# Hybrid streaming encoder step on one core: the last superchunk of the down projection in six, sixteen and six units, its norm on two engines, and the norm's shift added in memory

## The reference

```python
h = x @ w_in                       # branches: RG-LRU, band attention, forgetting attention
y = concat(rms(y_A), rms(y_B), rms(y_C))
x = LN1(ALPHA * x + y @ w_out)
hdn = square(relu(x @ w_up))       # 2048 -> 8192
out = LN2(ALPHA * x + hdn @ w_down)   # 8192 -> 2048; LN(v) = (v - mean) * rstd * g + b
```

## Time and profile before

| | us |
|---|---|
| median of 3 runs | 2359.68 (2357.44 to 2361.64) |
| profiled execution | 2353.08 |
| its span | 2351.3 |
| TensorE busy | 2294.7 (98%) |
| VectorE busy | 1558.3 (66%) |
| ScalarE busy | 955.2 (41%) |
| POOL busy | 264.1 (11%) |
| granted TensorE clock, mean | 0.995 |

### The profile page before, as it was taken

The page is one execution under the profiler, slowest core; times in us unless marked ns, Lnnn a source line. Parts: engine busy times, 40 slices in busy tenths (PEclk is TensorE's granted clock), DMA queues, the critical chain, the costliest instruction groups (busy, mean ns, idle before and its releaser), DMA issues. The chain is left out here.

```text
span 2351.3 us, 39849 instructions
## 1 busy us (share of the span) xinstructions
PE 2294.7 (98%) x16967; PEld 2250.5 (96%) x16967; DVE 1558.3 (66%) x1181; ACT 955.2 (41%) x957; POOL 264.1 (11%) x296
## 2 busy tenths in 40 slices
PE   7999999999999999999999999999999999998986
PEld 7999999999888999999999999999999999998985
DVE  3311455533457676667777777778778778778868
ACT  3222344423445354654444444455245235234332
POOL 2010233300011202200000000002112112111100
PEclk9999999999999999999999999999999999999998
DMA  7264333344643567775445555579689689769873
GB/s 211 82 193 128 104 101 101 97 153 132 194 150 109 162 207 231 215 245 191 154 156 182 160 178 182 170 236 239 174 238 247 180 235 238 197 184 273 205 224 117
DMA packets 383510, 421.99 MB, mean 179 GB/s; under 512 B 13716, under 2 KB 359512, under 8 KB 382824
## 3 DMA queue, kind: packets, MB, share of 16 engines
q1 hardware_dynamic: 319936, 335.73, 45.4%
q0 software_dynamic: 27552, 48.17, 10.8%
q10 hardware_dynamic: 35912, 36.49, 4.5%
HBM read 339.47 MB, written 82.45 MB: 179 GB/s over the span
## 5 line engine op out<-in xcount | busy, mean ns | idle before, releaser
L2506 PE MATMUL psum<-x_e_hi,w_hi 128*128 128x288 f32 x1600 | 471.4, 295 | 8.6 <-DVE w_lo L1703 7.0
L2506 PE MATMUL psum<-x_e_lo,w_hi 128*128 128x288 f32 x1600 | 472.7, 295 | 0.0
L2506 PE MATMUL psum<-x_e_hi,w_lo 128*128 128x288 f32 x1600 | 472.2, 295 | 0.0
L2506 PE MATMUL psum<-x_b_hi,w_hi 128*128 128x288 f32 x1536 | 452.9, 295 | 6.8 <-DVE w_lo L1821 2.7
L2506 PE MATMUL psum<-x_b_lo,w_hi 128*128 128x288 f32 x1536 | 453.8, 295 | 0.0
L2506 PE MATMUL psum<-x_b_hi,w_lo 128*128 128x288 f32 x1536 | 453.5, 295 | 0.0
L440 DVE TENSOR_TENSOR w_lo<-raw,w_hi 128x2048 fp32r<-128x2048 f32 x64 | 152.4, 2382 | 277.1 <-ACT w_hi L436 276.5
L2506 PEld LDWEIGHTS psum<-x_e_hi,w_hi 128*128 128x128 f32 x1600 | 301.5, 188 | 10.5 <-DVE w_lo L1703 8.6
L2506 PEld LDWEIGHTS psum<-x_e_lo,w_hi 128*128 128x128 f32 x1600 | 301.4, 188 | 0.0
L2506 PEld LDWEIGHTS psum<-x_e_hi,w_lo 128*128 128x128 f32 x1600 | 301.4, 188 | 0.0
L2506 PEld LDWEIGHTS psum<-x_b_hi,w_hi 128*128 128x128 f32 x1536 | 289.5, 188 | 8.9 <-DVE w_lo L1821 3.5
(11 more groups left out here) (390 smaller groups left out, 3786.4 us busy)
## 6 DMA issues: line engine op xcount, KB each, us to landing
raw<-in_w_down SPq DMA_DIRECT2D x62, 1024.0 KB, 7.1
raw<-in_w_up SPq DMA_DIRECT2D x54, 1024.0 KB, 6.6
raw<-in_w_in SPq DMA_DIRECT2D x40, 1024.0 KB, 5.3
a_even<-in_w_down SPq DMA_DIRECT2D x30, 1024.0 KB, 7.3
raw<-in_w_out SPq DMA_DIRECT2D x24, 1024.0 KB, 5.4
a_even<-in_w_up SPq DMA_DIRECT2D x24, 1024.0 KB, 6.7
h_scratch<-c_tile ACTq DMA_DIRECT2D x48, 288.0 KB, 2.8
down_scratch<-c_tile POOLq DMA_DIRECT2D x44, 288.0 KB, 5.7
```

What stands on the lines that cost most here:

```text
L2506: mm = pe.matmul(PS[:, bank, 0:HALF], w, x[:, k, :], start=(k + n == 0), stop=(k == UK - 1 and n == 2))
```

## The change

The last superchunk gets six first units, of which the last two take F2 for column blocks 0 and 1 (P_F), and six last units (P_E). Their weights, copies and accumulates follow; the load of S10F moves behind those of the first units 1 and 2. In the last block `lo_e(0)` comes ahead of the combination of HE1, and the combination after the two additions into Y1. Transposes follow half units instead of whole ones. `shift` is gone: VectorE makes `gain`, ScalarE multiplies by rstd (`scale`), and the shift ln2_b is written early, broadcast, to y_prompt and y_sample by two DMAs on ScalarE's queue; the rows are then accumulated onto it by POOL's DMAs.

```diff
-N_E = N_F + 5 * N_BLOCK
+N_E = N_F + 6 + 4 * N_BLOCK
-AFTER = ((0, 1, 2), (3, 4, 5), (6, 7), (8, 9), (10,), (11, 12), (13,), (14,))
+AFTER = (((0,), (1, 2)), ((3,), (4, 5)), ((6,), (7,)), ((8,), (9,)), ((10,), (11,)), ((12, 13), (14,)))
+P_F = ((0, 0), (0, 1), (0, 2), (0, 3), (1, 0), (1, 1))
+P_E = ((0, 2), (0, 3), (1, 0), (1, 1), (1, 2), (1, 3))
...
         def tile_e(v):
-            return 4 * (v % 4) + 2 * (v // 4)
+            return 4 * P_E[v][1] + 2 * P_E[v][0]
+        def tile_f(a):
+            return tile_a(N_SUPER, a, 0) if a < 4 else (CQ[a % 2], cd_out[a % 2], 16 * (7 * N_SUPER + 2))
...
@@ sync
             sp.dma_start(HB01[:, :, :], h_factor(0, 1, su)).then_inc(part_in[1], 16)
-            sp.wait_ge(lo_done, n + 1 + 3)
-            sp.wait_ge(sig, 4 * g + 4)
             sp.wait_ge(unit_done, n + 2 + 3)
             sp.dma_start(HE7[:, :, :], h_factor(1, 1, su)).then_inc(part_in[2], 16)
-            sp.dma_start(S10F[0][:, :, :], down_unit(1, 0, su, 0)).then_inc(a10_in, 16)
             sp.wait_ge(lo_done, n + 4 + 3)
             weights_f(1)
             sp.wait_ge(lo_done, A + 3)
             weights_f(2)
-            sp.dma_start(S11[0][:, :, :], down_unit(1, 1, su, 0)).then_inc(a11_in, 16)
+            sp.dma_start(S10F[0][:, :, :], down_unit(1, 0, su, 0)).then_inc(a10_in, 16)
             sp.wait_ge(lo_done, A + 1 + 3)
             weights_f(3)
+            sp.wait_ge(sig, 4 * g + 4)
+            sp.dma_start(S11[0][:, :, :], down_unit(1, 1, su, 0)).then_inc(a11_in, 16)
             sp.wait_ge(lo_done, A + 2 + 3)
+            weights_f(4)
+            sp.wait_ge(lo_done, A + 3 + 3)
+            weights_f(5)
+            sp.wait_ge(lo_done, A + 4 + 3)
             sp.dma_start(A00[:, :, :], down_unit(0, 0, su, 0)).then_inc(a00_in, 16)
...
             sp.wait_ge(unit_done, n + 2 + 3)
-            load_y0(0)
             sp.wait_ge(lo_done, N_E + 3)
             weights_e(2)
-            load_y0(1)
+            load_y0(2)
             sp.wait_ge(lo_done, N_E + 1 + 3)
             weights_e(3)
-            load_y0(2)
             load_y0(3)
-            for v in range(4, 8):
+            for v in (4, 5):
                 sp.wait_ge(lo_done, N_E + v - 2 + 3)
                 weights_e(v)
-            for n in range(4):
...
-                sp.dma_start(y_prompt[128 * t:128 * t + 128, c], ROWS_0[:, t, c]).then_inc(out_rows, 16)
+                load_y0(v - 4)
@@ scalar
             act.dma_start(s_fl, LFT[0:DEC, 4, :]).then_inc(stores, 16)
+            act.dma_start(y_prompt, ln2_b.to_broadcast([SEQ, D])).then_inc(shift_out, 16)
+            act.dma_start(y_sample, ln2_b.to_broadcast([DEC, D])).then_inc(shift_out, 16)
...
-            for a in range(4):
+            for a in range(6):
                 g, n, _ = block_f(0)
-                if a < 2:
+                if a < 4:
                     hi_a(su, a + 2)
                 else:
-                    hi_1b(n + a - 2, a % 2, (SIG2F, S10F[1])[a % 2], 4 * g + (2, 1)[a % 2])
-                tile, out, free_at = tile_a(su, a, 0)
+                    hi_1b(n + a - 4, a % 2, (SIG2F, S10F[1])[a % 2], 4 * g + (2, 1)[a % 2])
+                tile, out, free_at = tile_f(a)
...
+            def scale(h, t, c=slice(0, D)):
+                act.wait_ge(row_rs, 2 - h)
+                act.wait_ge(row_g, 3 * (1 - h) + t + 1)
+                w, r = ROW_T[t][1], row_tile(h, t)[:, c]
+                act.activation(r, r, ACT.Identity, scale=RST[0:w, 3 * h + t:3 * h + t + 1]).then_inc(row_y, 1)
-            for v in range(8):
-                if v < 6:
-                    hi_e(v + 2)
+            for v in range(6):
                 if v == 3:
                     row_sds(1, 1)
-                for s in AFTER[v]:
+                for s in AFTER[v][0]:
                     rows_copy(s)
+                if v < 4:
+                    hi_e(v + 2)
+                else:
+                    scale(1, v - 4)
+                for s in AFTER[v][1]:
+                    rows_copy(s)
+            scale(1, 2)
             rows_copy(15)
             row_sds(2, 0)
+            for t in range(2):
+                for n in range(2):
+                    scale(0, t, slice(D // 2 * n, D // 2 * (n + 1)))
+            scale(0, 2)
@@ vector
             combine(e1, e1, b01, 4 * su + 7)
+            lo_a(su, 4)
+            factor_rest(F6, HE6, 7 * su + 12)
+            lo_a(su, 5)
             dve.wait_ge(unit_done, N_F + 2)
             sigma1_f(g, 0)
+            factor_rest(F5, HE1, 7 * su + 13)
             sigma2_f(g, 0)
-            factor_rest(F6, HE6, 7 * su + 12)
+            factor_rest(F7, HE7, 7 * su + 11)
             lo_1b(n, 0, SIG2F)
-            factor_rest(F5, HE1, 7 * su + 13)
             sigma3_f(g, 0)
             lo_1b(n + 1, 1, S10F[1])
-            factor_rest(F7, HE7, 7 * su + 11)
...
                 else:
-                    dve.wait_ge(part_in[3], 16 * (2 * su + 3))
-                    combine(HE1[:, :, :], HE1[:, :, :], HB10_F[:, :, :], 4 * su + 8, minus=True)
-                    lo_e(0)
                     dve.wait_ge(part_in[0], 16 * (su + 3))
                     dve.wait_ge(post, p + 3)
                     dve.tensor_tensor(Y1[:, 14:16, :], Y1[:, 14:16, :], CQ[1][:, :, :], ALU.add).then_inc(y1_added, 1)
+                    lo_e(0)
...
                     dve.tensor_tensor(Y1[:, 12:14, :], Y1[:, 12:14, :], CQ[0][:, :, :], ALU.add).then_inc(y1_added, 1)
+                    dve.wait_ge(part_in[3], 16 * (2 * su + 3))
+                    combine(HE1[:, :, :], HE1[:, :, :], HB10_F[:, :, :], 4 * su + 8, minus=True)
                     lo_e(1)
                     factor_rest(F4F, HE1, 7 * su + 14)
...
+            for v in range(3):
+                add_y0(v)
+                lo_e(v + 2)
+                for s in ((0,), (1, 2, 3), (4, 5, 6))[v]:
                     row_stats(s)
+            row_stats(7)
+            row_means(1, 1)
+            add_y0(3)
+            lo_e(5)
+            row_rstd(1, 1)
+            dve.wait_ge(gb_in, 16)
+            gain(1, 0)
+            row_stats(8)
+            add_y0(4)
+            gain(1, 1)
+            row_stats(9)
+            row_stats(10)
+            gain(1, 2)
+            for s in range(11, 14):
+                row_stats(s)
+            add_y0(5)
+            row_stats(14)
             row_stats(15)
             row_means(2, 0)
-            gain(0, 0).then_inc(row_g, 1)
+            gain(0, 0)
             row_rstd(2, 0)
+            gain(0, 1)
+            gain(0, 2)
@@ gpsimd
             pool.dma_start(GR[:, :], ln2_g.to_broadcast([128, D])).then_inc(gb_in, 16)
-            pool.dma_start(BR[:, :], ln2_b.to_broadcast([128, D])).then_inc(gb_in, 16)
+            pool.wait_ge(shift_out, 32)
+            def add_out_rows(h, t, n, dst, p0=0, p1=None, c=slice(0, D)):
+                p1 = ROW_T[t][1] if p1 is None else p1
+                pool.wait_ge(row_y, n)
+                pool.dma_start(dst[:, c], row_tile(h, t)[p0:p1, c], accum_op=ALU.add).then_inc(out_rows, 16)
...
@@ tensor
+                    for s in AFTER[v][m]:
+                        rows_transposed(s)
```

More of the change, by code:

```diff
@@ L352, in encoder_step @@
         stats_done, row_sd, row_rs = sem("stats_done"), sem("row_sd"), sem("row_rstd")
-        row_g, row_y, out_rows, out_rows_p = (sem(n) for n in ("row_gain", "row_y", "out_rows", "out_rows_first"))
+        row_g, row_y, out_rows = (sem(n) for n in ("row_gain", "row_y", "out_rows"))
+        shift_out = sem("row_shift_out")
         class Chain:
@@ L769, in load_y1 @@
                 for i in range(2):
[L770 removed]
+                    sp.wait_ge(cd_out[i], 16 * (7 * su + (0 if b == N_BLOCK - 1 else 3 + b + 1)))
                 src = YD[4 * b:4 * b + 4, :, HALF:TOK].rearrange("k p c -> p k c")
@@ L2076, in row_rstd, with add_y0 @@
                 dve.wait_ge(row_rs, n)
-            for v in range(8):
+            def add_y0(v):
+                i, b = P_E[v]
                 for m in range(2):
                     dve.wait_ge(*((unit_done, N_E + v + 3) if m else (d_m0, v + 1)))
-                    dve.wait_ge(y0_in[v % 4], 16)
+                    dve.wait_ge(y0_in[b], 16)
                     at = Y0[:, tile_e(v) + m, :]
-                    dve.tensor_tensor(at, at, PS[:, 2 * m + v % 2, 0:HALF], ALU.add if v < 4 else ALU.subtract).then_inc(d_ev[m], 1)
-                if v < 6:
-                    lo_e(v + 2)
-                for s in AFTER[v]:
-                    row_stats(s)
-                if v == 2:
-                    row_means(1, 1)
-                elif v == 3:
-                    row_rstd(1, 1)
-                    dve.wait_ge(gb_in, 32)
-                    chain(gain(1, 0))
-                elif v == 4:
-                    shift(1, 0).then_inc(row_y, 1)
-                    chain(gain(1, 1))
-                elif v == 5:
-                    shift(1, 1).then_inc(row_y, 1)
-                elif v == 6:
-                    chain(gain(1, 2))
```

(25 more changed lines are left out.)

70 lines of the change are left out of this document (36 added, 34 removed).

## The result

| | before | after |
|---|---|---|
| median of 5 runs, us | 2358.72 (2357.44 to 2361.64) | 2370.35 (2367.99 to 2373.54) |
| ratio, 95% interval | | 1.0048 (1.0034 to 1.0061) |
| profiled execution (span), us | 2353.08 (2351.3) | 2368.42 (2366.6) |

The change makes the kernel 11.6 us slower by the medians. The forecast was 2361.5 with a range to 2368, so it was wrong, and beyond its range. The two profiled executions differ by 15.3 us. Three places carry that, and a fourth part is scatter.

A forecast was written before the change was run, and what follows sets the result against it. TensorE, busy 98% of the span, was taken as the bound, so its idle time and the tail count. -2.7 - 4.1 + 8.6 = +1.8 gave 2361.5 us against the 2359.7 median; range 2351.5 to 2368, the forecast's own 2356 to 2365.

The forecast's parts named there:

- first units: Last superchunk's start: both waits for L1821 (1.9 us) and about 0.25 of matmul tail go, -2.7 us in all.
- last units and output: From the last block unit's end to the span's end: 76.7 us against 80.8, -4.1 (range -7.5 to -2.8).
- copies at the gates: Shift copies on ScalarE's queue delay w_ra and w_rx: stall of 7.0 plus 1.65 of slow clock, +8.6 us.
- the stall of 3.5 us ahead of the block: Before the last superchunk's first block TensorE still waits for VectorE's low-part chain: 3.5 us where 3.8 was.
- the new wait behind ScalarE's order: ScalarE waits for HE1's combination before last unit 1's high part; that unit starts at B+10.4, not B+7.6.
- the time of the copies: Shift copies ahead of the gates: 4.72 MB at x_lo's 390 GB/s take 12.1 us, the gates stall 7.0.
- rival B: Copies within memory run at 252 GB/s, w_rx lands at 269.0, gates lose 11.6: +6.5, 2366.2 us; chance 0.20.
- The slow stretch behind the stall: After the gates' stall TensorE runs at a lower granted clock, costing 1.65 us.
- the 5 us that I drew from it: Gate stall if DMA engines share rings by packets only, small weight rows beside 8 KB rows: 5 us rather than 7.
- Rival A: The gates do not wait, copies being overtaken or much quicker; only the tail counts: -6.8, 2352.9 us; chance 0.24.
- the output: Final row accumulates by POOL: they end at B+76.5 (B: last block unit's end), plus 0.2 to the span's end.
- my own upper end: Final accumulates: 2.36 MB moving from B+65.4 at 184 GB/s would end at B+78.2 (B: last block unit's end).

The follow-up runs named there:

- copies alone: Kernel before, with only the two memory-to-memory copies of the shift added at the head of ScalarE's queue: 2374.3 us, 16.6 over the kernel before (ratio 1.0067).
- half: Kernel before plus the copies at the head of ScalarE's queue, the first cut to y_prompt[256:SEQ, :], 2560 KB instead of 4608: 2366.38 us, 7.9 over (1.0028).

## Why the prediction was wrong

| term, us | predicted | between the two profiles |
|---|---|---|
| first units | -2.7 | -3.0 |
| last units and output | -4.1 | +0.5 |
| copies at the gates | +8.6 | +16.0 |
| start of the program, and 300 to 2120 us | 0 | -1.7 and +3.4 |
| sum | +1.8 | +15.2 |

The first units came out as worked out, to the stall of 3.5 us ahead of the block. Of the last units, the steps that concern the engines hold too: the new wait behind ScalarE's order is there, last unit 1 starts at B+10.5 (predicted 10.4), TensorE comes to its wait at B+51.0 (50.4), the first gain ends at B+63.0 (62.1; the last transposes took 1.5 us at the lower clock instead of 0.85), the last scale ends at B+69.8 (68.9).

**The step that failed first** is the time of the copies: "at the rate of x_lo (4.72 MB plus one weight load of 1.05 in 14.7 us, 390 GB/s) they take 12.1 us ... a stall of 7.0". The rate of a store from SBUF was put on a copy within memory; the run that really stores from SBUF has 400 GB/s and a stall of 8.3, the copies have 275 to 330 GB/s and 13.2. The stall was 6.2 us longer than I had it, in three pieces. From the copies' first packet (249.7) to their last the bytes took some 16.3 us where I had 14.4, although the weights beside them were 0.52 MB, half of what I had allowed for. The small loads then took another 3 us, to 269.0, in turns with the packets of the raw weights; I had nothing for them. And in this execution the gates were due at 255.9, 1.5 us sooner, while the copies moved only 0.3 sooner: 3.4 us after their issue and not 1.9. My rival B had the size right, from the 252 GB/s of the earlier trace rows, the only rows of the trace with copies of that kind. The nearer row in kind stood there and I preferred the nearer row in bytes, and gave B 0.20. But that B's w_rx at 269.0 is the measured one to a tenth is luck: the copies moved at 290 GB/s, and the loads' own 3 us, which B lacks too, made up for it.

The slow stretch behind the stall was too small as well: 1.65, from the stall of 3.8 us in the earlier trace rows (where 14.49 less 12.74 is in fact 1.75), against 2.8 here. In the other runs it cost 1.8 behind a stall of 12.2 (copies alone), 2.3 behind 8.6 (on GpSimd's queue), 2.5 behind 8.3 (from SBUF) and 2.4 behind 5.3 (half): it does not follow the stall's length.

The rule of the Trainium skill that I quoted, turns by packets, held here, and with it the smaller part for the weights' small rows; the 5 us that I drew from it failed by the rate. The about 358 GB/s of the Trainium skill, which stand in the section Where 436 GB/s comes from of that page, would have given copies of 26 us if counted for reading and for writing; the bytes moved in 16.3.

The mechanism was right for this kernel, and only its size was off: the gates waited because ScalarE's queue kept its order, as the packets show. It was not the whole danger. With the copies on GpSimd's queue the wait is still 8.6 us, by turns of one packet with the small stores ahead of the loads, of which I had not thought. The run with the same copies behind the landing of those weights shows that the place decides. Rival A (the gates don't wait) was wrong in this kernel, and its sign came in that one.

**The second** is the output: "I take B+76.5, near the accumulates"; it was B+81.3, beyond my own upper end of 78.2. The rate was right (184 GB/s predicted, 175 to 207 measured). My upper end was the last byte at B+78.2 (-2.6 by the sum, not the -2.8 given), and I went below it without a row for that. The first accumulate is issued at B+64.6, the bytes run to B+78.7, the last landing is at B+79.3, and 2.0 us more, for which I had 0.2, lie between it and the end. Plain stores in the same kernel end it 5.9 us earlier, so that the reordered tail with plain stores would have given what I forecast and more (without the shift in its outputs, though). So 5.2 us less arithmetic at the end brought nothing: the accumulates gave it back.

The rest is scatter between executions. The medians differ by 11.6 us, the profiles by 15.3. Two of my kernels that are the same up to the last units have their last block's end 6.9 us apart (VectorE's first read of it at 2269.4 and 2276.3), with 7.8 us in 8 waits for low parts in the one and 10.3 in 15 in the other. That is 2.5 of the 6.9; where the rest comes from was not traced. By the medians, the measured 11.6 is the copies' 16.6 less 5 for the rest; the run with the copies in eight pieces gives 1 to 3 for the same rest. The medians tell it no closer.

## What to carry to other kernels

Before a large transfer is added in a "quiet" stretch, list what is issued in the 20 us beside it on any queue, how many packets stand ahead of it there, and when it is wanted: 4.7 MB cost 14 to 17 us ahead of two 64 KB loads, and nothing when issued 6 us later, behind them. Price a copy within memory and an accumulate by rows of their own kind (copies here some 290 GB/s of payload while moving and 240 from issue to landing, accumulates 190, plain stores 400). Accumulates are good for results with work still ahead of them; the last results of a kernel should leave by plain stores.

## What the runs showed of the hardware that was not expected

- Queues took turns of one packet, whatever its size: 608 packets of 16 bytes, which had passed in under 2 us with the engines free, took 12 beside packets of 8 KB of another queue, and the small loads behind them in their own queue landed after 17.3 us instead of 2.0 (median of the same load).
- A queue that joined while another filled the engines began late: 3.6 us from issue to the first packet (ScalarE's small stores beside the copies on GpSimd's queue), 5.0 (SyncE's raw weights in the changed kernel), at least 3.4 (plain stores beside accumulates).
- A plain store of 512 KB landed after 2.7 us beside other plain stores, and after 7.2 beside accumulates on another queue.
- The first matmuls after the stall of 13 us ran at the lower clock for some 5.4 us (269.1 to 274.5), although TensorE was then busy without a pause. The slow clock cost 2.8 us there, 2.4 behind a stall of 5.3 us, and 1.8 behind one of 12.2.
- Where transfers of GpSimd's queue landed last, the span ended 2.0 and 2.1 us after the landing (accumulates, plain stores); with SyncE's plain stores last, 0.4.
